# Decoder trunk: the last two sums of each scan visit on GpSimd, and dense gate and up columns side by side

## The chip, the cores and the metric

One core of a Trainium2 chip runs the whole kernel. The metric is device time in microseconds, the median of several executions. TensorE multiplies matrices, VectorE (DVE), ScalarE (ACT) and GpSimd (POOL) work elementwise, and SyncE (SP) issues the weight transfers. PSUM has eight banks of 512 float32 columns per partition.

## What is computed

Two layers of a hybrid decoder trunk over 256 tokens of width 1024. Each layer normalises its input, projects it, runs three token mixers (a diagonal state-space scan, dilated attention, attention into 256 memory tokens), merges them and adds the residual. Then comes a channel mixer: dense SwiGLU in layer 0, top-2-of-8 experts in layer 1. Two pieces matter here:

```python
def ssm_branch(u, ...):            # 32 groups x 64 complex states
    bu = jnp.einsum('blgc,gpc->blgp', uf.astype(jnp.complex64), b_bar)
    ...
    _, states = lax.associative_scan(combine, (a_el, bu), axis=1)
    y = jnp.einsum('blgp,gcp->blgc', states, c).real + d_skip * uf
...
def swiglu(h, w_gate, w_up, w_down):      # dense: 1024 -> 2816 -> 1024
    return (jax.nn.silu(h @ w_gate) * (h @ w_up)) @ w_down
```

## The kernel before

The engines run programs of their own, written out by hand, and meet at named semaphores. Matrix products of weights are split: a float32 weight tile of 128x2048 is copied by ScalarE to a rounded part `hi` (`hi_part`, line 1351), VectorE forms `lo` = tile - `hi` (`lo_part`, line 1897), and TensorE does three products per block (`split_product`, lines 583 to 585). A ring of three tiles (`ring`) is filled by SyncE (`load`, line 400), 1 MB per tile; `hi` and `lo` have three buffers each.

**The scans (`ssm`).** The states are turned into a rotating frame, scanned with real factors, and turned back. A layer has 8 visits v, each over two state blocks of 128 and both parts, real and imaginary. VectorE per visit: two products of the PSUM input with the cosine and sine tables (lines 1697, 1698, 128x1024), two sums (1704, 1705, 128x512), four scans (1708), two products to turn back (1711, 1712), two sums that write the states to `wv[v % 2]` (1713, 1714), and after some visits a skip path (1725). It waits for `states_ready` of the visit before at the head of each visit. TensorE per visit: `rotated_input(v + 1)` (line 704), one part of the input projection in plain float32 (line 618), then `state_output(v)` (line 717), which waits for `states_ready`. The input of visit v + 1 goes to the same banks as that of visit v and waits for `bu_used`.

**After the scans.** VectorE does the rotary products and head scaling, then the lo parts `ring_lo` (line 1545). ScalarE does squares of the memory keys, GELU, the key scaling (line 1241), a copy of the input, two weight copies `hi_m` (line 1110), then copies of transposed heads and the column block. GpSimd forms inverse roots (`rsqrt_mean`, lines 534 and 535): of q and k (`rqk`), then of the memory keys (`rm`). TensorE transposes the heads and goes on with split products.

**The dense part (`dense`).** The 2816 hidden columns are done in 11 blocks f of 256. A gate tile and an up tile have all 1024 rows of 256 columns each, a down tile 256 rows of 1024 columns. TensorE in the loop: gate of block f + 1 into bank 0 (two token halves of 256 columns side by side), transposes of block f's activations into bank 2, up of block f + 1 into bank 1, down of block f into banks 4 to 7. ScalarE does silu (line 1378) when gate is done, so while up is multiplied; VectorE multiplies by up (line 1936). The first block uses banks 0 and 1 for gate, 2 and 3 for up, because its first half starts before the second half of the input is transposed.

In all of it each engine takes its instructions in the order of its program.

## Time and profile before

| What | Value |
|---|---|
| Median of 3 runs | 1869.81 us (1869.48 to 1870.22) |
| Profiled execution, its own time | 1874.48 us |
| Its span from first to last instruction | 1872.6 us |
| TensorE busy | 97% |
| VectorE busy | 78% |
| ScalarE busy | 60% |
| GpSimd busy | 2% |
| Mean granted clock of TensorE | 0.988 |

The busy share counts a matmul from its start to its modelled end, and successive ones overlap; the pace is read from starts. The scans of layer 0 run from 68 to 149 us, those of layer 1 from 588 to 668, the dense part from 335 to 529, and the experts from about 870 to the end.

### The profile page before, as it was taken

How to read it: one execution, taken by the hardware profiler on the slowest of the kernel's cores; microseconds unless marked ns; L12 is line 12 of the kernel's file. 1: busy time of each engine (PE TensorE's matmuls, PEld its weight loads, DVE VectorE, ACT ScalarE, POOL GpSimd, SP SyncE). 2: the span in 40 equal slices, each digit the busy share in tenths (PEclk: the TensorE clock that was granted, in tenths of full speed). 3: DMA queues.
4: the chain of work that ended last, by engine and by line, in shares of the span. 5: the costliest groups of instructions: out<-in, count | busy, mean ns of one | idle time of the engine just before them, and what ended most of it. 6: DMA issues, size and time to landing. Idle time of an engine off the chain costs nothing.

```text
span 1872.6 us, 24006 instructions
## 1 busy us (share of the span) xinstructions
PE 1822.3 (97%) x8731; PEld 1441.1 (77%) x8731; DVE 1469.5 (78%) x1320; ACT 1130.0 (60%) x1211; POOL 43.7 (2%) x83
## 2 busy tenths in 40 slices
PE   7999999999999999998999999999999999999997
PEld 5445888999974458877888888888888888888886
DVE  7997456554469985466889898898888888988986
ACT  5336464544342364645677776776777767767774
POOL 1002000000010020000000000000000000000000
PEclk9999999999999999998999999999999999999999
DMA  6333334655543334456999999999999999999994
GB/s 215 121 113 126 128 128 154 205 176 169 194 152 113 113 113 135 127 170 228 348 369 332 370 369 329 371 349 352 373 326 365 367 338 369 350 350 369 352 372 178
DMA packets 226956, 476.48 MB, mean 254 GB/s; under 512 B 15644, under 2 KB 40344, under 8 KB 226904
## 3 DMA queue, kind: packets, MB, share of 16 engines
q1 hardware_dynamic: 226520, 474.99, 71.9%
q0 software_dynamic: 288, 0.79, 0.2%
q8 instruction: 33, 0.54, 0.1%
q14 instruction: 19, 0.16, 0.0%
q10 hardware_dynamic: 96, 0.02, 0.0%
HBM read 474.71 MB, written 1.05 MB: 254 GB/s over the span
## 4 chain that ended last, share of the span: by engine, by line
PE 60%; DVE 6%; issue 1%; ACT 0%; DVEq 0%; ACTq 0%
PE ps L583 18%; PE ps L585 18%; PE ps L584 18%; PE ps L968 2%; PE ps L989 1%; DVE z L1708 1%; DVE lo L1897 1%; DVE x L2052 1%; PE ps L784 1%; PE ps L756 1%; DVE z L1711 0%; DVE z L1698 0%; DVE z L1712 0%; PE ps L1054 0%; PE ps L1053 0%
## 5 line engine op out<-in xcount | busy, mean ns | idle before, releaser
L1897 DVE TENSOR_TENSOR lo<-ring_e,hi 128x2048 fp32r<-128x2048 f32 x336 | 767.5, 2290 | 110.8 <-ACT hi L1351 110.5
L1351 ACT ACTIVATE hi<-ring_e 128x2048 fp32r<-128x2048 f32 x336 | 644.1, 1918 | 185.3 <-PE ps L585 185.1
L583 PE MATMUL ps<-hi,xe_hi 128*128 128x512 f32 x896 | 355.6, 397 | 2.2 <-DVE lo L1897 2.0
L585 PE MATMUL ps<-hi,xe_lo 128*128 128x512 f32 x896 | 349.4, 390 | 0.0
L584 PE MATMUL ps<-lo,xe_hi 128*128 128x512 f32 x896 | 349.3, 390 | 0.0
L618 PE MATMUL ps<-ring,hT 128*128 128x512 f32 x448 | 200.7, 602 | 0.0
L583 PEld LDWEIGHTS ps<-hi,xe_hi 128*128 128x128 f32 x896 | 168.2, 188 | 39.4 <-DVE lo L1897 5.7
L585 PEld LDWEIGHTS ps<-hi,xe_lo 128*128 128x128 f32 x896 | 168.2, 188 | 36.3
L584 PEld LDWEIGHTS ps<-lo,xe_hi 128*128 128x128 f32 x896 | 168.4, 188 | 33.2
L583 PE MATMUL ps<-hi,aT_hi 128*128 128x512 f32 x464 | 181.6, 391 | 0.0
L585 PE MATMUL ps<-hi,aT_lo 128*128 128x512 f32 x464 | 180.7, 390 | 0.0
L584 PE MATMUL ps<-lo,aT_hi 128*128 128x512 f32 x464 | 180.7, 389 | 0.0
L1110 ACT ACTIVATE hi_m<-ring 128x2048 fp32r<-128x2048 f32 x52 | 99.5, 1914 | 118.4 <-PE ps L585 109.8
L618 PEld LDWEIGHTS ps<-ring,hT 128*128 128x128 f32 x448 | 84.0, 192 | 104.0 <-issue 103.9
L583 PE MATMUL ps<-hi_m,xT_hi 128*128 128x512 f32 (+1 forms) x368 | 147.1, 400 | 5.8 <-DVE ring_lo L1545 5.7
L584 PE MATMUL ps<-ring_lo,xT_hi 128*128 128x512 f32 (+1 forms) x368 | 141.3, 384 | 0.0
L1545 DVE TENSOR_TENSOR ring_lo<-ring,hi_m 128x2048 fp32r<-128x2048 f32 x52 | 118.7, 2286 | 22.5 <-ACT hi_m L1110 22.4
L585 PE MATMUL ps<-hi_m,xT_lo 128*128 128x512 f32 (+1 forms) x304 | 116.3, 382 | 0.0
L1118 ACT ACTIVATE z<-ps,rs 128x512 f32<-128x512 f32 (+1 forms) x52 | 31.9, 667 | 134.4 <-PE ps L618 134.4
L583 PE MATMUL ps<-hi,hT_hi 128*128 128x256 f32 x352 | 100.6, 286 | 1.4 <-DVE lo L1897 1.4
L585 PEld LDWEIGHTS ps<-hi,aT_lo 128*128 128x128 f32 x464 | 87.1, 188 | 18.4
L584 PEld LDWEIGHTS ps<-lo,aT_hi 128*128 128x128 f32 x464 | 87.2, 188 | 17.5
(311 smaller groups left out, 2499.4 us busy)
## 6 DMA issues: line engine op xcount, KB each, us to landing
ring_e<-in_moe_w_gate SPq DMA_DIRECT2D x112, 1024.0 KB, 6.8
ring_e<-in_moe_w_up SPq DMA_DIRECT2D x112, 1024.0 KB, 6.9
ring_e<-in_moe_w_down SPq DMA_DIRECT2D x112, 1024.0 KB, 6.6
ring<-in_w_in SPq DMA_DIRECT2D x50, 1024.0 KB, 5.1
ring<-in_ffn_w_gate SPq DMA_DIRECT2D x11, 1024.0 KB, 5.3
ring<-in_ffn_w_up SPq DMA_DIRECT2D x11, 1024.0 KB, 6.3
ring<-in_ffn_w_down SPq DMA_DIRECT2D x11, 1024.0 KB, 4.9
ring<-in_w_mem_kv SPq DMA_DIRECT2D x8, 1024.0 KB, 6.4
```

Source lines behind the costliest of these rows:

```text
L583: nc.tensor.matmul(o, x_hi, w_hi, start=first, stop=False, skip_group_check=True)
L584: nc.tensor.matmul(o, x_hi, w_lo, start=False, stop=False, skip_group_check=True)
L585: return nc.tensor.matmul(o, x_lo, w_hi, start=False, stop=end, skip_group_check=True)
L618: last = nc.tensor.matmul(o, lhs[0][:, kk, t], w[:, k, :], start=first, stop=end, skip_group_check=True)
L756: last = nc.tensor.matmul(ps[:, bank, col:col + nk], qkT[o:o + HD, 0, hd // 2, c * P:(c + 1) * P], qkT[o:o + HD, 1, hd // 2, 0:nk], start= ...
L784: last = nc.tensor.matmul(ps[:, 5, o:o + v.shape[1]], pT[:, b * P:(b + 1) * P], v, start=first, stop=end, skip_group_check=True)
L968: last = nc.tensor.matmul(ps[:, 6 + half, k % KT * P:(k % KT + 1) * P], h[:, c, k * P:(k + 1) * P], disp[:, c, :], start=c == 0, stop=c == ...
L1110: nc.scalar.activation(hi_m[:, m % 2, :], ring[:, n % R, :], ACT.Copy).then_inc(sem("mixer_hi_ready"), 1)
L1118: last = nc.scalar.activation(dst[:, c, :], ps[:, pair + c, 0:dst.shape[2]], ACT.Copy, scale=rs[:, 2 + c:3 + c])
L1351: nc.scalar.activation(hi[:, m % H, :], src, ACT.Copy).then_inc(sem("hi_ready"), 1)
L1545: V.tensor_tensor(ring_lo[:, n % R, :], ring[:, n % R, :], hi_m[:, m % 2, :].bitcast(F32), ALU.subtract).then_inc(sem("mixer_lo_ready"), 1)
L1897: last = V.tensor_tensor(lo[:, m % H, :], src, hi[:, m % H, :].bitcast(F32), ALU.subtract)
```

## The change

In the scans, VectorE's last two sums go to GpSimd. VectorE writes the cosine product to a new buffer `wc` and the sine product over `wp`, and signals `states_turned`; GpSimd forms both sums into `wv[v % 2]` and signals `states_ready`. VectorE's wait for `states_ready` of the visit before moves from the head of a visit to its scans, which overwrite `wp`.

In the dense part a tile now holds 512 of the 1024 rows, with 256 gate columns beside 256 up columns, and comes in two transfers with a semaphore each (`full`, `up_full`). One matmul covers gate and up of one row block, 512 columns wide; each token half has a bank of its own (0 and 1). The second block goes to banks 2 and 3, with the first block's transposes in bank 0. TensorE's loop is: transposes of block f, both halves of block f + 1, down of block f. Silu and product follow the end of both halves.

```diff
-        wa, wb, wp, *wv = [z[:, i // 3, SSM_COLS * BANK + i % 3 * 4 * SEQ:SSM_COLS * BANK + (i % 3 + 1) * 4 * SEQ]
-                           .rearrange("p (i r t) -> p i r t", i=2, r=2) for i in range(5)]
+        wa, wb, wp, wc, *wv = [z[:, i // 3, SSM_COLS * BANK + i % 3 * 4 * SEQ:SSM_COLS * BANK + (i % 3 + 1) * 4 * SEQ]
+                           .rearrange("p (i r t) -> p i r t", i=2, r=2) for i in range(6)]
...
                         sp.wait_ge(sem(name), count + (0 if n < BASE[1] + R else {"columns_done": COL_TILES}.get(name, MIDDLE)))
-                v = ring[:, n % R, :].rearrange("p (k n) -> p k n", n=src.shape[2])
-                sp.dma_start(v, src).then_inc(full[n % R], 16)
+                v = ring[:, n % R, :].rearrange("p (k n) -> p k n", k=blocks_ or src.shape[1])
+                sp.dma_start(v[:, :, cols_], src).then_inc(full[n % R], 16)
+                return v
...
+                    def load_pair(n, f, half, shift=0):
+                        rows = slice(half * KT * P, (half + 1) * KT * P)
+                        gate, up = (w[0][rows, bass.ds(f * 256, 256)].rearrange("(k p) n -> p k n", p=P)
+                                    for w in (ffn_gate, ffn_up))
+                        v = load(n, gate, shift, KT, slice(0, 256))
+                        sp.dma_start(v[:, :, 256:BANK], up).then_inc(up_full[n % R], 16)
...
-                    load(n0, gate_tile(ffn_gate, 0))
-                    load(n0 + 1, gate_tile(ffn_up, 0))
-                    load(n0 + 2, gate_tile(ffn_gate, 1))
-                    load(n0 + 3, gate_tile(ffn_up, 1))
+                    load_pair(n0, 0, 0)
+                    load_pair(n0 + 1, 0, 1)
+                    load_pair(n0 + 2, 1, 0)
+                    load_pair(n0 + 3, 1, 1)
                     load(n0 + 4, down_tile(0))
                     with sp.Fori(2, NF) as f:
-                        load(n0 + 5, gate_tile(ffn_gate, f), f - 2)
-                        load(n0 + 6, gate_tile(ffn_up, f), f - 2)
+                        load_pair(n0 + 5, f, 0, f - 2)
+                        load_pair(n0 + 6, f, 1, f - 2)
                         load(n0 + 7, down_tile(f - 1), f - 2)
                     load(n0 + 3 * NF - 1, down_tile(NF - 1))
...
+                for v in range(NJ // 2):
+                    w = wv[v % 2]
+                    pool.wait_ge(sem("states_turned"), NJ // 2 * l + v + 1)
+                    nc.gpsimd.tensor_tensor(w[:, :, 0, :], wc[:, :, 0, :], wp[:, :, 1, :], ALU.subtract)
+                    nc.gpsimd.tensor_tensor(w[:, :, 1, :], wc[:, :, 1, :], wp[:, :, 0, :], ALU.add).then_inc(
+                        sem("states_ready"), 1)
...
             def dense():
-                def hidden(bank, m, shift):
-                    w_hi, w_lo = split_tile(m, 256, shift)
+                def hidden(m, half, shift=0, between=None, bank=0):
+                    w_hi, w_lo = split_tile(m, BANK, shift)
                     for c in range(C):
-                        for k in range(KD):
-                            last = split_product(ps[:, bank, c * 256:(c + 1) * 256], hT_hi[:, k, c * P:(c + 1) * P],
-                                                 hT_lo[:, k, c * P:(c + 1) * P], w_hi[:, k, :], w_lo[:, k, :],
-                                                 k == 0, k == KD - 1)
+                        for k in range(KT):
+                            kk, tt = half * KT + k, slice(c * P, (c + 1) * P)
+                            last = split_product(ps[:, bank + c, :], hT_hi[:, kk, tt], hT_lo[:, kk, tt], w_hi[:, k, :],
+                                                 w_lo[:, k, :], kk == 0, kk == KD - 1)
+                        if c == 0 and between is not None:
+                            between()
                     last.then_inc(sem("split_used"), 1)
...
-                def step(f, shift, first, between=None):
-                    pe.wait_ge(sem("silu_done"), f)
-                    hidden(0, 2, shift)
+                def step(f, shift, between=None):
                     act_transposes(f)
-                    hidden(1, 3, shift)
-                    down(f, 4, shift, first, False, between)
-                def hidden_half(bank, m, half):
-                    w_hi, w_lo = split_tile(m, 256)
...
                 pe.wait_ge(sem("transposed_used"), batches_to(0, "ffn") - 2)
-                hidden_half(0, 0, 0)
-                block_pairs(x, KT, KD, (sem("x_mixed"), 1))
-                hidden_half(2, 1, 0)
+                hidden(0, 0, between=lambda: block_pairs(x, KT, KD, (sem("x_mixed"), 1)))
                 pe.wait_ge(sem("transposed_used"), batches_to(0, "ffn"))
-                hidden_half(0, 0, 1)
-                hidden_half(2, 1, 1)
-                step(1, 0, True)
+                hidden(1, 1)
+                hidden(2, 0, bank=2)
+                act_transposes(1, 0)
+                hidden(3, 1, bank=2)
+                down(1, 4, 0, True, False)
                 with pe.Fori(2, NF - 1) as f:
-                    step(f, 3 * (f - 1), False)
-                step(NF - 1, 3 * (NF - 2), False, NF)
+                    step(f, 3 * (f - 1))
+                step(NF - 1, 3 * (NF - 2), NF)
                 down(NF, FFN_TILES - 1, 0, False, True, lhs=(end_hi, end_lo))
...
-                def silu(gate_done, first=False):
+                def silu(gate_done, bank=0):
                     act.wait_ge(sem("split_used"), gate_done)
                     for c in range(C):
                         o = slice(c * 256, (c + 1) * 256)
-                        last = nc.scalar.activation(gate_act[:, o], ps[:, c, 0:256] if first else ps[:, 0, o], ACT.Silu,
+                        last = nc.scalar.activation(gate_act[:, o], ps[:, bank + c, 0:256], ACT.Silu,
                                                     scale=rs[:, 2 + c:3 + c])
                     last.then_inc(sem("silu_done"), 1)
...
-                    nc.scalar.activation(dst[:, 0:BANK], ps[:, 2, :], ACT.Copy).then_inc(sem("aT_hi_ready"), 1)
-                def step(f, s, wait_act):
-                    split(2, s)
-                    split(3, s)
-                    if wait_act:
+                    nc.scalar.activation(dst[:, 0:BANK], ps[:, bank, :], ACT.Copy).then_inc(sem("aT_hi_ready"), 1)
+                def step(f, s, first=False):
+                    if not first:
                         act.wait_ge(sem("split_used"), 3 * f - 1)
-                    act_hi(f)
+                    act_hi(f, bank=0 if first else 2)
                     split(4, s)
+                    split(5, s, pair=f + 1)
                     act.wait_ge(sem("act_ready"), f)
-                    silu(3 * f)
-                split(2, 0, False)
+                    silu(3 * f + 1, 2 if first else 0)
+                    split(6, s, pair=f + 2)
+                split(2, 0, False, 1)
                 act.wait_ge(sem("x_rs"), 2)
-                silu(1, True)
-                split(3, 0)
-                act_hi(1)
-                split(4, 0)
-                act.wait_ge(sem("act_ready"), 1)
-                silu(3)
+                silu(2)
+                split(3, 0, pair=2)
+                step(1, 0, True)
                 for k in range(KD):
                     last = nc.scalar.activation(xT_hi[:, k, :], memT[:, k, :], ACT.Copy, scale=gains[:, 1, 1, k:k + 1])
                 last.then_inc(sem("memory_hi_ready"), 1)
-                with act.Fori(2, NF) as f:
-                    step(f, f - 1, True)
+                with act.Fori(2, NF - 1) as f:
+                    step(f, f - 1)
+                act.wait_ge(sem("split_used"), 3 * NF - 4)
+                act_hi(NF - 1)
+                split(FFN_TILES - 2, 0)
+                act.wait_ge(sem("act_ready"), NF - 1)
+                silu(3 * NF - 2)
...
                     bu = ps[:, 4:6, :].rearrange("p j (r t) -> p j r t", r=2)
-                    if v > 0:
-                        dve.wait_ge(sem("states_ready"), NJ // 2 * l + v)
                     dve.wait_ge(sem("bu_done"), NJ // 2 * l + v + 1)
                     V.tensor_tensor(wa[:], bu, spread(cos, 2, 2), ALU.mult)
                     last = V.tensor_tensor(wb[:], bu, spread(sin, 2, 2), ALU.mult)
...
+                    if v > 0:
+                        dve.wait_ge(sem("states_ready"), NJ // 2 * l + v)
                     for i in range(2):
                         for r in range(2):
                             last = V.tensor_tensor_scan(wp[:, i, r, :], spT[:, 0, j + i:j + i + 1].to_broadcast([P, SEQ]),
                                                         w[:, i, r, :], 0.0, ALU.mult, ALU.add)
                     chain(last)
-                    V.tensor_tensor(wa[:], wp[:], spread(cos, 2, 2), ALU.mult)
-                    chain(V.tensor_tensor(wb[:], wp[:], spread(sin, 2, 2), ALU.mult))
-                    V.tensor_tensor(w[:, :, 0, :], wa[:, :, 0, :], wb[:, :, 1, :], ALU.subtract)
-                    V.tensor_tensor(w[:, :, 1, :], wa[:, :, 1, :], wb[:, :, 0, :], ALU.add).then_inc(
-                        sem("states_ready"), 1)
+                    chain(V.tensor_tensor(wc[:], wp[:], spread(cos, 2, 2), ALU.mult))
+                    V.tensor_tensor(wp[:], wp[:], spread(sin, 2, 2), ALU.mult).then_inc(sem("states_turned"), 1)
                     if v >= 2 and v % 2 == 0:
...
-                        last = V.scalar_tensor_tensor(out=act_out[:, o], in0=ps[:, 2 + c, 0:256] if first else ps[:, 1, o],
+                        last = V.scalar_tensor_tensor(out=act_out[:, o], in0=ps[:, bank + c, 256:BANK],
                                                       scalar=rs[:, 2 + c:3 + c],
                                                       in1=gate_act[:, o], op0=ALU.mult, op1=ALU.mult)
                     last.then_inc(sem("act_ready"), 1)
...
-                dense_product(1, 2, True)
-                def step(f, s):
-                    split(3, s)
-                    act_low(f)
+                dense_product(1, 2)
+                split(3, 0)
+                def step(f, s, first=False):
+                    act_low(f, bank=0 if first else 2)
                     split(4, s)
-                    dense_product(f + 1, 3 * f + 1)
-                step(1, 0)
+                    split(5, s)
+                    dense_product(f + 1, 3 * f + 1, 2 if first else 0)
+                    split(6, s)
+                step(1, 0, True)
                 dve.wait_ge(sem("memory_hi_ready"), 1)
                 for q in range(0, KD, 2):
                     last = memory_low(1, q)
                 last.then_inc(sem("memT_scaled"), 1)
-                with dve.Fori(2, NF) as f:
-                    split(2, f - 1)
+                with dve.Fori(2, NF - 1) as f:
                     step(f, f - 1)
+                act_low(NF - 1)
+                split(FFN_TILES - 2, 0)
+                dense_product(NF, 3 * NF - 2)
                 split(FFN_TILES - 1, 0)
                 act_low(NF, end_hi, end_lo)
                 weights_low(1, 2)
```

## Rows read from the trace of the kernel before

**Rows 1.** The page, part 1: busy time of each engine

```profile
PE 1822.3 (97%) x8731; PEld 1441.1 (77%) x8731; DVE 1469.5 (78%) x1320; ACT 1130.0 (60%) x1211; POOL 43.7 (2%) x83
```

**Rows 2.** timeline, TensorE, dense part: start, us, engine, line, shapes, [idle <-releaser]

```profile
394.84 0.28 PE L585 MATMUL ps<-hi,hT_lo 128*128 128x256 f32 x1
...
396.28 0.28 PE L585 MATMUL ps<-hi,hT_lo 128*128 128x256 f32 x1
396.40 0.40 PE L583 MATMUL ps<-hi,aT_hi 128*128 128x512 f32 x1
...
401.64 0.39 PE L585 MATMUL ps<-hi,aT_lo 128*128 128x512 f32 x1
```

**Rows 3.** timeline of ScalarE and VectorE in one dense step

```profile
497.68 0.83 ACT L1378 ACTIVATE gate_act<-ps,rs 128x256 f32<-128x256 f32 x2
...
501.08 1.92 ACT L1351 ACTIVATE hi<-ring 128x2048 fp32r<-128x2048 f32 x1 [0.77 <-PE ps L585]
...
501.17 0.88 DVE L1936 SCALAR_TENSOR_TENSOR act_out<-ps,rs,gate_act 128x256 f32<-128x256 f32 x2 [1.06 <-PE ps L585]
501.96 2.28 DVE L1897 TENSOR_TENSOR lo<-ring,hi 128x2048 fp32r<-128x2048 f32 x1
```

**Rows 4.** timeline of TensorE and ScalarE, first block of the dense part

```profile
339.75 0.39 PE L583 MATMUL ps<-hi,hT_hi 128*128 128x256 f32 x1 [0.58 <-DVE lo L1897]
...
345.85 1.28 ACT L1378 ACT_TABLE_LOAD   x1 [1.64 <-PE ps L585]
```

**Rows 5.** timeline, VectorE, one scan visit and the start of the next

```profile
98.21 1.22 DVE L1697 TENSOR_TENSOR z<-ps,costab 128x1024 f32<-128x1024 f32 x1
...
101.92 2.44 DVE L1708 TENSOR_TENSOR_SCAN z<-spT,z 128x256 f32<-128x256 f32 x4
...
106.79 0.69 DVE L1713 TENSOR_TENSOR z<-z 128x512 f32<-128x512 f32 x1
...
108.12 1.23 DVE L1697 TENSOR_TENSOR z<-ps,costab 128x1024 f32<-128x1024 f32 x1
```

**Rows 6.** timeline, TensorE: outputs (L717) and inputs (L704) of scan visits, both layers

```profile
92.27 1.06 PE L717 MATMUL ps<-z,cT 128*32 128x256 f32 x8
...
128.84 1.06 PE L717 MATMUL ps<-z,cT 128*32 128x256 f32 x8
130.62 1.14 PE L704 MATMUL ps<-uT,bT 32*128 32x256 f32 x8 [0.71 <-DVE z L1698]
...
148.42 1.06 PE L717 MATMUL ps<-z,cT 128*32 128x256 f32 x8 [1.53 <-DVE z L1714]
...
601.80 1.06 PE L717 MATMUL ps<-z,cT 128*32 128x256 f32 x8
...
668.38 1.06 PE L717 MATMUL ps<-z,cT 128*32 128x256 f32 x8 [1.53 <-DVE z L1714]
```

**Rows 7.** timeline of GpSimd, and VectorE beside it at 135.5 us

```profile
5.11 0.40 POOL L529 TENSOR_SCALAR_AFFINE_SELECT mask<-mask 128x256 f32<-128x256 f32 x1
...
136.17 0.69 POOL L534 TENSOR_SCALAR rqk<-rqk 128x48 f32<-128x48 f32 x1 [112.52 <-ACT hi_m L1226]
136.94 8.43 POOL L535 TENSOR_TENSOR rqk<-rqk,half_neg 128x48 f32<-128x48 f32 x1
...
151.24 2.36 POOL L535 TENSOR_TENSOR rm<-rm,half_neg 128x8 f32<-128x8 f32 x1
...
135.54 1.22 DVE L1712 TENSOR_TENSOR z<-z,sintab 128x1024 f32<-128x1024 f32 x1
```

**Rows 8.** timeline of ScalarE and TensorE after the scans, layer 0

```profile
161.50 1.91 ACT L1110 ACTIVATE hi_m<-ring 128x2048 fp32r<-128x2048 f32 x1 [1.44 <-DMA ring<-in_w_in]
...
169.92 0.47 PE L583 MATMUL ps<-hi_m,xT_hi 128*128 128x512 f32 x1 [0.59 <-DVE ring_lo L1545]
```

**Rows 9.** busy time by window: PE, PEld, DVE, ACT, POOL, granted clock, DMA

```profile
170.00:174.00 4.00, 4.00 (x11) 3.15 (x12) 1.98 (x1) 3.30 (x19) 0.53 (x2) 0.57 0.00 0
```

**Rows 10.** transfers by source: count, KB each, median us to landing

```profile
ring<-in_ffn_w_up SPq DMA_DIRECT2D x11, 1024.0 KB, 6.3
```

38 lines of the change are left out of this document (18 added, 20 removed).

## The prediction

> **What bounds the kernel now.** I began with the page. TensorE is busy for 97% of the span and no other engine for more than 78% [rows 1]. So a microsecond is won only where TensorE itself becomes shorter, or where it stands still. VectorE and ScalarE count only where TensorE waits for them. The change touches two places, and I read the timeline of each.
>
> In the dense part the reader should look at start times, not durations, since matmuls overlap in the records. Thirteen 256-column matmuls stand between 394.84 and 396.28 with equal steps, so one costs 1.44 / 12 = 0.120 us. The 24 matmuls of 512 columns of the down product run from 396.40 to 401.64, 5.24 / 23 = 0.228 us each [rows 2]. Twice 0.120 is 0.240: the wide form does the same columns in 0.012 us less. No gap separates them; TensorE sets the pace there. ScalarE and VectorE wait for it: 0.77 us before a hi copy, 1.06 us before the product of gate and up [rows 3].
>
> In the scans it is VectorE that sets the pace. One visit starts at 98.21, the next at 108.12, a cadence of 9.91 us without a gap [rows 5]. TensorE's share of a visit is less: from the output of visit 1 at 92.27 to that of visit 5 at 128.84 are four visits, 9.14 us each. It starts behind VectorE, catches up, and stands still in the end, 1.53 us before the last output in both layers [rows 6].
>
> **The scans, part by part.** VectorE loses the last two sums. From the first of them at 106.79 to the next visit at 108.12 are 1.33 us [rows 5], so its visit falls to 9.91 - 1.33 = 8.58 us, below TensorE's 9.14. If GpSimd keeps up, TensorE becomes the bound, and the gain is what it stands still now. Layer 0: from output 5 to output 7 it takes 148.42 - 128.84 = 19.58 us; two visits without a wait are 18.28, less the input matmuls that the last one lacks, 1.14 with its overlap, 1.07 net, 17.21. Gain 2.4 us. Layer 1: 668.38 - 601.80 = 66.58 against 7 x 9.14 - 1.07 = 62.91. Gain 3.7 us [rows 6].
>
> Does GpSimd keep up? Its sums of 128x512 with two operands have no row. The nearest is a one-operand pass over 256 columns in 0.40 us [rows 7]. Below, one sum can't be under that 0.40; above, four times its columns (512, two operands) give 1.6. I take 1.2, since part of the 0.40 is a fixed cost. The far end is the pass over 48 columns that took 0.69 [rows 7]: by width, 7.4 us per sum. I don't take it for a rate, since it began at 136.17, within VectorE's multiply that ran from 135.54 for 1.22 us, and it ended 0.10 after that one [rows 7]: it was held up.
>
> The wait for the sums moves from the head of the next visit to its scans. VectorE has 101.92 - 98.21 = 3.71 us of other work before it [rows 5]: the two products from PSUM and the two input sums. Two GpSimd sums at 1.2 plus some 0.2 for the semaphores are 2.6, so nothing waits; even at 1.6 it is 3.4. Cover is gone above 1.75 us per sum. What would queue behind the wait are the scans, the turning back, and the input matmuls of the visit after next, which need VectorE's next products. The output matmuls get their states 2.6 - 1.33 = 1.3 us later within a visit. For the last visit of layer 0: its input matmuls start at 130.62 less the 0.71 they wait now, and are done at 131.0 [rows 6]; 8.58 for VectorE and 2.6 for GpSimd give 142.2, and TensorE asks at 148.42 - 2.4 = 146.0.
>
> A rule of the Trainium skill speaks against this part. By "SBUF — State Buffer", Who interferes with whom, a VectorE instruction with two SBUF inputs contends with a GpSimd instruction that reads SBUF, and the one that comes first keeps the port for all of its duration. The held-up pass above agrees. By that rule the sums run free beside the two products that read PSUM, for 2.4 us, and the first input sum, which reads SBUF twice, starts just then: it would lose 0.1 us or nothing. The Trainium skill's "GPSIMD Engine Reference", Elementwise — side-by-side cycle accounting, gives 4497 ns for 2048 columns of such a sum; by width that is an estimate of 1.1 us for these, and with it the sum of this part stays the same.
>
> GpSimd's queue is in order, and behind the visits stand the head norms. Now the pow over q and k starts at 136.94, in the middle of the scans; then its two passes, 0.69 + 8.43, start at 142.2 and end at 151.3 [rows 7]. VectorE wants it only behind its rotary products, which start after the last output, at 147. The memory keys' norm follows: a short pass (0.4) and 2.36. It ends at 154.1, today at 151.24 + 2.36 = 153.6 [rows 7], so in layer 0 ScalarE's key scaling starts no earlier than now. In layer 1 (520 us later now, by 668.38 - 148.42) the last input matmuls end at 601.80 + 5 x 9.14 + 2.1 = 649.6, the sums at 660.8, the norm at 672.7 against 673.6: 0.9 earlier. That chain has 1.44 us of idle before its second weight copy, for a transfer that TensorE will now release earlier, and what it hands to TensorE comes 0.6 us early: TensorE's last wait before the split weights is 0.59 us, for VectorE [rows 8]. So VectorE's chain would give the whole 2.4 and 3.7, ScalarE's no more than 1.44 + 0.6 = 2.0 in layer 0 and 0.9 + 2.0 = 2.9 in layer 1. The later chain decides. Sum of the scans: 4.9 us.
>
> **The dense part, part by part.** 1056 matmuls of 256 columns become 528 of 512 (11 blocks, 48 each), on the same operands. 528 x (0.240 - 0.228) = 6.3 us [rows 2]. In the rows a fixed cost of 12 ns per matmul is what the halving saves (0.240 - 0.228). The Trainium skill's "TensorE: Matmul & The Clock Gate", Back-to-back issue gap, puts that fixed cost at 2.5 ns when the clock is warm; by it the halving would give an estimated 528 x 2.5 ns = 1.3 us.
>
> The price is that gate and up end together, so silu and product come one after the other, behind both tile halves. With T the end of the hidden product: silu 0.83, product 0.88 and semaphores, done at T + 1.9 [rows 3]. TensorE then does the down product, 24 x 0.228 = 5.5 us, and only after it wants the transposes: 3.6 us of cover. The bank that silu reads is written again only after those. The third copy of a step follows silu: hi 1.92, lo 2.28, done at T + 5.2 [rows 3], wanted at T + 11.3. Its slot is then loaded in 6.3 us [rows 10] to T + 11.5, wanted by ScalarE at T + 16.8. SyncE issues two transfers for each of 22 tiles instead of one, 22 more, of half the size and with the same row length; its queue mostly waits for lo parts, so they cost nothing while that slack of 5 us stands.
>
> The first block: TensorE's 0.58 us for the second tile's lo part [rows 4] goes, because 12 wide matmuls now stand before that tile is wanted instead of none after the transposes. In its place: tile 3's hi copy stands behind the first silu. From the end of block 0: table load 1.28 [rows 4], silu 0.83, hi 1.92, lo 2.28, semaphores 0.2, together 6.5 us; TensorE comes at 24 x 0.228 + 0.4 for the transposes = 5.9. New wait 0.6. The banks of the second block's own remove the wait for that first silu, which would be 2.2 us. At the end, the last down product waits for silu, hi, transposes and both copies in a row: by the same durations 0.1 to 0.2 us. Sum of the dense part: 6.3 + 0.6 - 0.6 - 0.15 = 6.1 us.
>
> **The sum.** 4.9 + 6.1 = 11.0 us. The profiled execution took 1874.48 us (span 1872.6), which becomes 1863.5. The median of the runs is 4.67 below it; I take the difference over: 1869.81 - 11.0 = 1858.8 us. The expert stage, the larger half of the span, keeps every instruction and only starts earlier.
>
> One cost can fall either way. At 170 us TensorE is granted 0.57 of its clock on average for 4 us, mostly the lower of its two levels [rows 9], which costs 4 x 0.43 = 1.7 us; the same spot in layer 1 keeps the full clock. The first may vanish, or the second appear: 1.7 us to both sides.
>
> **Rivals.** (a) The scans give nothing: a sum takes around 2.3 us, or the chain behind the scans swallows it. For it: the norms now queue behind the sums. Against: 3.71 us of cover, and idle in both chains. Time 1869.8 - 6.1 = 1863.7. (b) The dense part gives nothing: the wide form keeps the narrow one's pace per column, 0.240, or silu and product don't fit under the down product. Against: the wide form at 0.228 stands beside the narrow one in one stretch [rows 2], and the cover is 3.6 us. Time 1869.8 - 4.9 = 1864.9. The Trainium skill's 2.5 ns (TensorE page, as above) would put this case 1.3 us lower. (c) Slower: the sums on GpSimd become the bound. A visit is then two sums, 0.2, and 106.79 - 101.92 = 4.87 from the scans on [rows 5]. At 2.4 us per sum that is 9.9, today's cadence, and the last output also comes 2.4 + 2.4 + 0.2 - 1.33 = 3.7 later; less skips that it hides, about 2.7 per layer. So from about 2.5 us per sum the loss exceeds the dense part's 6.1. At 3 us a visit is 11.1: 8.58 + 7 x 11.1 + 6.2 = 92.5 against 80 now, 12 per layer, 1869.8 + 25 - 6.1 = 1888. The 0.69 for 48 columns speaks for it, its end just behind VectorE's against [rows 7].
>
> **How the numbers follow.** Forecast 75%, (a) 11%, (b) 9%, (c) 3%, and 2% for what I don't see. The forecast's own range takes the whole stall in both layers (1.2 more), the clock (1.7 both ways), and 0.5 to 1.5 for the small waits of the dense part: 1855.0 to 1862.5. To hold 8 in 10 with bounds it reaches to (a) and (b): 1855.0 to 1865.0. This measurement can tell about 0.2%, 3.7 us, from no change: faster is below 1866.1. All but (c) and a part of (a) and (b) lie there: faster 0.92, same 0.05, slower 0.03.
>
> **What would show it.** Right: wide matmuls 0.228 apart and steps 16.8 us apart where transposes start; GpSimd sums near 1.2 us; VectorE never waiting before a scan; outputs 9.1 us apart up to the last, at about 146.0 and 664.7; the split weights after the scans 2 to 3 us earlier. Wrong: sums over 1.75 us, VectorE's input sums stretched by the port, a wait before transposes or lo parts in each dense step, or ScalarE's key scaling late for the norm by more than its idle.

## The result and the profile after

The changed kernel takes 1855.23 us (median of 4 runs, 1853.55 to 1856.46), beside 1869.81 for the kernel before. The ratio is 0.9917, with the interval 0.9905 to 0.9929: 13.3 to 17.8 us less, where I had forecast 11.0. A second measurement of the same kernel on another chip gave 1856.21 us beside 1871.26, ratio 0.9922 (0.9908 to 0.9936). Both medians of the kernel before leave out its slow runs, one of 7232.69 us in the first measurement and two of 2027.84 and 2277.74 us in the second. Applied to the 1869.81 us of the forecast the first ratio gives 1854.3 us, 0.7 below the lower end of my range.

The profiled execution took 1854.96 us, with a span of 1853.1. The page of the changed kernel, part 1, answers to [rows 1]:

```profile
PE 1808.8 (98%) x8203; PEld 1409.6 (76%) x8203; DVE 1451.9 (78%) x1288; ACT 1130.7 (61%) x1211; POOL 81.9 (4%) x115
```

TensorE has 528 instructions fewer, VectorE 32 fewer, GpSimd 32 more. Next the timeline of TensorE, outputs of the scan visits in both layers, as in [rows 6]:

```profile
80.88 1.06 PE L730 MATMUL ps<-z,cT 128*32 128x256 f32 x8
90.00 1.06 PE L730 MATMUL ps<-z,cT 128*32 128x256 f32 x8
...
135.64 1.06 PE L730 MATMUL ps<-z,cT 128*32 128x256 f32 x8
...
585.11 1.06 PE L730 MATMUL ps<-z,cT 128*32 128x256 f32 x8
...
647.93 1.06 PE L730 MATMUL ps<-z,cT 128*32 128x256 f32 x8
```

The outputs are 9.12 us apart and none waits: TensorE sets the pace of the scans now, as forecast. From first to last are 62.8 us in both layers. One visit on GpSimd and VectorE, in place of [rows 5]:

```profile
102.41 1.27 POOL L559 TENSOR_TENSOR z<-z 128x512 f32<-128x512 f32 x1 [6.47 <-DVE z L1721]
103.64 1.27 POOL L560 TENSOR_TENSOR z<-z 128x512 f32<-128x512 f32 x1
...
103.38 1.22 DVE L1705 TENSOR_TENSOR z<-ps,sintab 128x1024 f32<-128x1024 f32 x1
104.63 0.83 DVE L1711 TENSOR_TENSOR z<-z 128x512 f32<-128x512 f32 x1
105.38 0.68 DVE L1712 TENSOR_TENSOR z<-z 128x512 f32<-128x512 f32 x1
106.09 2.44 DVE L1717 TENSOR_TENSOR_SCAN z<-spT,z 128x256 f32<-128x256 f32 x4
```

A sum takes GpSimd 1.27 us; I took 1.2. VectorE's scan waits for nothing. But its first input sum (L1711) takes 0.83 us, not 0.69: it begins at 104.63, and GpSimd's second sum runs until 104.91. That is so in four of the eight visits; in three others a skip path stands ahead of VectorE's next products, and the first has no sums beside it, and there it takes 0.69. This small delay becomes important below.

The dense part on TensorE and ScalarE, as in [rows 2, 4]:

```profile
346.18 0.50 PE L596 MATMUL ps<-hi,hT_hi 128*128 128x512 f32 x1 [0.52 <-DVE lo L1903]
...
396.76 0.39 PE L596 MATMUL ps<-hi,hT_hi 128*128 128x512 f32 x1
...
402.65 0.39 PE L598 MATMUL ps<-hi,aT_lo 128*128 128x512 f32 x1
```

```profile
339.86 1.28 ACT L1387 ACT_TABLE_LOAD   x1 [3.21 <-PE ps L598]
341.16 0.84 ACT L1387 ACTIVATE gate_act<-ps,rs 128x256 f32<-128x256 f32 x2
341.88 1.92 ACT L1358 ACTIVATE hi<-ring 128x2048 fp32r<-128x2048 f32 x1
```

The 26 steps from 396.76 to 402.65 are 0.2265 us each (5.89 / 26), and the new wait for the fourth tile, 0.6 by the forecast, is 0.52, behind table load, silu and hi copy in the order I gave. Besides that wait, the change costs time in one place, behind the scans of layer 1 (GpSimd, ScalarE, TensorE):

```profile
646.39 8.04 POOL L542 TENSOR_TENSOR rqk<-rqk,half_neg 128x48 f32<-128x48 f32 x1
654.52 0.63 POOL L541 TENSOR_SCALAR rm<-rm 128x8 f32<-128x8 f32 x1
655.23 2.23 POOL L542 TENSOR_TENSOR rm<-rm,half_neg 128x8 f32<-128x8 f32 x1
...
657.55 2.45 ACT L1246 ACTIVATE kv<-kv,rm 128x128 f32<-128x128 f32 x8 [2.31 <-POOL rm L542]
...
666.03 0.63 PE L584 MATMUL ps<-ident,kv 128*128 128x128 f32 x4 [1.35 <-ACT qkT L1091]
```

GpSimd's norms queue behind its sums, ScalarE waits 2.31 us for the last of them, and TensorE 1.35 us for ScalarE. From the last output to the first split product are 22.5 us there, 21.5 in layer 0 and in both layers of the kernel before.

### The profile page after: what moved, and what is told of

Read it like the earlier page. It is cut to its first block, busy times and chain, and to the rows that moved or that the text cites. A ratio compares the mean times of both kernels' runs of the same rounds, so it can differ in the third digit from the quotient of the medians.

```text
span 1853.1 us, 23022 instructions
## 1 busy us (share of the span) xinstructions
PE 1808.8 (98%) x8203; PEld 1409.6 (76%) x8203; DVE 1451.9 (78%) x1288; ACT 1130.7 (61%) x1211; POOL 81.9 (4%) x115
## 4 chain that ended last, share of the span: by engine, by line
PE 87%; DVE 8%; issue 2%; ACT 2%; POOL 1%; DMA 0%; DVEq 0%; ACTq 0%
PE ps L596 25%; PE ps L598 24%; PE ps L597 24%; PE ps L631 5%; PE ps L973 2%; PE ps L994 1%; PE ps L797 1%; DVE z L1717 1%; PE ps L769 1%; DVE lo L1903 1%; PE ps L584 1%; DVE x L2062 1%; PE ps L780 1%; DVE z L1720 1%; DVE z L1704 1%
## 5 line engine op out<-in xcount | busy, mean ns | idle before, releaser
L1903 DVE TENSOR_TENSOR lo<-ring,hi 128x2048 fp32r<-128x2048 f32 x33 | 75.6, 2292 | 44.0 <-ACT hi L1358 44.0
L597 PEld LDWEIGHTS ps<-lo,aT_hi 128*128 128x128 f32 x464 | 87.2, 188 | 17.8
```

The lines of the kernel that those rows point to most:

```text
L597: nc.tensor.matmul(o, x_hi, w_lo, start=False, stop=False, skip_group_check=True)
L1903: last = V.tensor_tensor(lo[:, m % H, :], src, hi[:, m % H, :].bitcast(F32), ALU.subtract)
```

## Where the time came from

The spans of the two profiled executions differ by 19.5 us, 4.9 more than the medians, since the profiled execution of the kernel before was one of its slower ones. So I compared it stage by stage with the changed kernel and three kernels of the experiments. Each stage starts where the engine that sets its pace starts (us, differences of start times):

```
stage                                   before  e4     e1     e2     after
                                                memory scans  dense
layer 0: VectorE's first product of the
  scans to first output (TensorE)       15.00   13.59  13.56  13.58  13.63
  ... to last output                    80.28   80.28  76.39  80.27  76.45
last output to first split product      21.50   21.50  21.50  21.50  21.50
first split to first hidden product    165.34  163.71 165.26 162.62 162.62
first hidden product to the down
  product behind the last one, dense   183.04  181.90 183.03 175.27 175.27
layer 1: VectorE's first product
  to first output                       13.69   12.19  13.68  13.49  12.19
  ... to last output                    80.27   80.27  76.50  80.27  75.01
last output to first split product      21.50   21.50  21.50  21.50  22.52
```

The row "to last output" is the finding. With VectorE as bound it is 80.27 or 80.28 us in every kernel with the old visit, whether TensorE's first output comes after 13.6 or after 15.0 us. With TensorE as bound it is the first output plus 62.8. In the profiled execution of the kernel before TensorE had a lower granted clock shortly ahead of both scans (a cold stretch, below), and was late. Busy time by window of the kernel before (columns as in [rows 9]):

```profile
36.00:44.00 8.00, 8.00 (x27) 6.12 (x28) 7.56 (x21) 2.44 (x7) 0.00 (x0) 0.79 0.26 100
...
588.00:600.00 12.00, 9.49 (x21) 4.42 (x22) 11.77 (x15) 7.51 (x4) 0.00 (x0) 0.72 0.23 86
```

and of the kernel of e4, which is the kernel before but for its memory copies:

```profile
36.00:44.00 8.00, 8.00 (x31) 5.54 (x31) 7.61 (x22) 2.80 (x6) 0.00 (x0) 1.00 0.45 156
588.00:592.00 4.00, 4.00 (x11) 1.70 (x8) 3.93 (x7) 4.00 (x4) 0.00 (x0) 0.58 0.02 4
592.00:600.00 8.00, 8.00 (x31) 3.59 (x30) 7.81 (x11) 0.60 (x2) 0.00 (x0) 1.00 0.17 44
```

My stall of 2.4 us was measured from an output that was itself 1.4 us late (15.00 against 13.59). The lateness cost the kernel before nothing, as VectorE's chain covered it, and so TensorE stood still that much less. By the stages the scans give 80.28 - 76.45 = 3.8 us in layer 0. In layer 1 they give 3.8 if TensorE is late there (e1), or 5.3 less the 1.0 behind the scans, 4.2, if not. The dense part gives 183.04 - 175.27 = 7.8. Together 15.4 to 15.8 us, against 14.6 and 15.1 between the medians. The rest of the 19.5 us belongs to the two executions, not to the change: 2.7 between the first split and the first hidden product of layer 0, where the granted clock of the kernel before was 0.79 and 0.78 from 168 to 176 us and 0.95 and 0.63 from 276 to 284, and 0.9 ahead of the scans. The first of these stages took 162.6 us in e2, 163.7 in e4 and 165.3 in e1 and in e10, so it goes with neither part of the change.

## The experiments

Ratios are to the kernel before on the same chip; intervals are 95%. Kernels e1 to e4 ran together, e5 to e8, and e9 to e12.

**e1: the scan part alone.** The kernel before with only the scan part of the change, its new buffer, its semaphore and the moved wait included. Its core:

```
-  V.tensor_tensor(w[:, :, 0, :], wa[:, :, 0, :], wb[:, :, 1, :], ALU.subtract)
-  V.tensor_tensor(w[:, :, 1, :], wa[:, :, 1, :], wb[:, :, 0, :], ALU.add)
+  nc.gpsimd.tensor_tensor(w[:, :, 0, :], wc[:, :, 0, :], wp[:, :, 1, :], ALU.subtract)
+  nc.gpsimd.tensor_tensor(w[:, :, 1, :], wc[:, :, 1, :], wp[:, :, 0, :], ALU.add)
...
```

> The kernel before with the scan part of the change alone (GpSimd forms the two last sums). Theory A (the parts are independent, and the scan part gives the net shifts that the changed kernel's trace showed, 2.46 us at the last output of layer 0 and 2.74 us up to the first product after the scans of layer 1): 5.1 us less, ratio 0.997 to the kernel before. Theory B (part of the gain of the whole change comes from TensorE's granted clock, or from the parts together, which neither part has alone): under 4 us or over 6.5 us less, with the cold stretches of this run elsewhere than at 170 and 280 us. GpSimd's sums 1.27 us each, VectorE's visit 8.7 us, outputs of the products 9.13 us apart in both.

Measured: 1863.88 us, ratio 0.9961 (0.9947 to 0.9974), 7.3 us less; 7.6 between the medians. Theory A's 5.1 is just inside the interval (4.9 to 9.9), but what it rests on was wrong: it took the shifts from the first output on. The stages of the table give 3.9 + 3.8 = 7.7. The size is theory B's, over 6.5, but not its cause: where the kernel before has a low granted clock at 168 and 276 us, this one has it at 164 and 272, the same places of its program, and between its first split and first hidden product it takes 165.26 us against 165.34. The gain is in the two scan stages.

**e2: the dense part alone.** The tile order, the 512-column products and the banks of the second block, on the kernel before.

> The kernel before with the dense part of the change alone (gate and up columns side by side, second block in banks of its own). Theory A (independent parts): 9 steps by 0.59 us from the wide products is 5.3, the wait of 0.87 to 1.17 us behind the memory copies in the second step gone, 1.3 in the first two blocks: 7.8 us less, ratio 0.996. My forecast's own sum for this part was 6.1 (ratio 0.9967). Theory B: what the measured 14.6 us holds beyond 5.1 + 7.8 = 12.9 is found here, 9 to 10 us less, if the clock of the dense part is what rose.

Measured: 1863.30 us, ratio 0.9964 (0.9950 to 0.9977), 6.7 us less by the ratio and 8.2 by the medians. Its stage is 175.27, as that of the whole change. The two parts add up: 7.7 and 7.8 in the traces, and 1 - 0.9961 + 1 - 0.9964 = 0.0075 against 0.0083 measured for both.

**e3: narrow products in the new order.** In the changed kernel each hidden product becomes two:

```
+  for n in range(2):
+      o = slice(n * 256, (n + 1) * 256)
+      ... split_product(ps[:, bank + c, o], ..., w_hi[:, k, o], w_lo[:, k, o], kk == 0 and n == 0, ...)
```

> The changed kernel with each 512-column hidden product of the dense part issued as two of 256 columns, gate and up, in the same banks and order of tiles. Theory A (a product costs its columns plus a fixed part of about 12 ns, so 528 more of them cost it 528 times): 5.3 to 6.4 us more than the changed kernel, ratio to the kernel before about 0.995. Rival (the gain of the dense steps came from the order of the tiles and the banks, not the width; fixed part of 2.5 ns): 0 to 1.3 us more than the changed kernel, ratio 0.992 to 0.993, and steps of the dense part within 0.15 us of 16.82 us.

Measured: 1862.52 us, ratio 0.9953 (0.9940 to 0.9967), 7.3 us over the changed kernel's first median and 6.3 over its second. The stage is 181.54 us, 6.3 more. In it TensorE's wait ahead of the fourth tile is 0.20 us, not 0.52, so that the products themselves cost 6.6 more, and 6.59 / 528 = 12.5 ns each. TensorE's timeline of this kernel, dense part:

```profile
395.78 0.28 PE L596 MATMUL ps<-hi,hT_hi 128*128 128x256 f32 x1
...
399.98 0.28 PE L598 MATMUL ps<-hi,hT_lo 128*128 128x256 f32 x1
```

That is 35 steps of 0.120. The width is the gain; the 2.5 ns that the rival took is not what is seen here. (The Trainium skill's "TensorE: Matmul & The Clock Gate", Back-to-back issue gap, gives that figure for the isolated gap, and says that in a stream of weight loads and products both set the spacing. These products have weights of their own each, and the trace shows 12.5 ns.)

**e4: the memory's copies spread over two steps.** In the kernel before:

```
-  for k in range(KD): last = nc.scalar.activation(xT_hi[:, k, :], memT[:, k, :], ...)
+  for part_ in range(2):
+      for k in range(part_ * KT, part_ * KT + KT): last = nc.scalar.activation(...)
+      if part_ == 0: step(2, 1, True)
...
```

VectorE's low parts of the memory are spread in the same way.

> The kernel before with the copies of the memory (high part on ScalarE, low part on VectorE) spread over two dense steps, four and four, in place of all eight in one. Theory (the wait of 0.87 us of TensorE for the low copies of a hidden tile, in the second dense step, comes from VectorE forming the memory's low copies for 3.25 us just before; the step has no other cause for it): the wait goes, 0.9 to 1.2 us less than the kernel before, ratio 0.9994. Rival (the wait comes from the tile's late load or from ScalarE's high copies, which are the same work in either place): the wait stays, no change within 0.3 us.

Its reason is a wait that I had missed. VectorE and TensorE in the kernel before, second dense step:

```profile
361.43 3.25 DVE L1563 SCALAR_TENSOR_TENSOR mem_lo<-memT,par,xT_hi 128x256 fp32r<-128x256 f32 x8
364.59 4.49 DVE L1897 TENSOR_TENSOR lo<-ring,hi 128x2048 fp32r<-128x2048 f32 x2
...
366.93 0.39 PE L583 MATMUL ps<-hi,hT_hi 128*128 128x256 f32 x1 [0.87 <-DVE lo L1897]
```

Measured: the wait is gone and the stage 181.90 us in place of 183.04, 1.1 less. The time, 1870.92 us, ratio 0.9996 (0.9987 to 1.0005), can't show so little. In the changed kernel the wait is gone too, since a step there is 12 wide products ahead of the next tile.

**e5 and e6: three and four sums per visit.** In the changed kernel GpSimd's first sum is done twice, or three times:

```
+  chain(nc.gpsimd.tensor_tensor(w[:, :, 0, :], wc[:, :, 0, :], wp[:, :, 1, :], ALU.subtract))
```

> The changed kernel with GpSimd's first sum of each visit done twice over: three sums in place of two. Theory A (cover of 3.7 us between VectorE's last product of a visit and its next input sum, and a visit that may last up to TensorE's 9.13 us): three sums with their wait take 3.9 to 4.0 us, VectorE waits 0.2 to 0.3 us, the visit lasts at most 9.0 us, outputs stay 9.13 us apart, under 1 us more than the changed kernel. Rival (the sums already bound the visit, as the rival of the prediction has it): 1.27 us by 16 visits by 2 layers less the first, 30 to 40 us more.

> The changed kernel with GpSimd's first sum of each visit done three times over: four sums in place of two. Theory A: the sums take 5.2 us or more against a cover of 3.7, the visit grows to about 10.2 us and passes TensorE's 9.13, so 7 visits by 1.1 us in each layer, 8 to 10 us at each last output: 15 to 20 us more than the changed kernel, outputs of the products 10.2 us apart. Rival (GpSimd's sums have more cover than 3.7 us, or VectorE doesn't wait for them): under 5 us more, outputs still 9.13 us apart.

Measured: e5 1876.81 us, ratio 1.0028 (1.0017 to 1.0039), 21.6 us over the changed kernel; e6 1895.76, ratio 1.0129 (1.0114 to 1.0145), 40.5 over. My theory fell: a third sum already costs more than the whole change gives. The rival's size, 30 to 40 us, wasn't met either. By the stages of the table, e5 loses 6.0 and 7.4 us up to the last outputs and 4.4 and 3.4 behind them. VectorE doesn't wait for the third sum by a semaphore. Its own sum stands still. VectorE and GpSimd in e5:

```profile
97.13 1.21 DVE L1706 TENSOR_TENSOR z<-ps,sintab 128x1024 f32<-128x1024 f32 x1
98.37 1.78 DVE L1712 TENSOR_TENSOR z<-z 128x512 f32<-128x512 f32 x1
100.08 0.68 DVE L1713 TENSOR_TENSOR z<-z 128x512 f32<-128x512 f32 x1
...
97.11 1.27 POOL L560 TENSOR_TENSOR z<-z 128x512 f32<-128x512 f32 x1
98.34 1.27 POOL L561 TENSOR_TENSOR z<-z 128x512 f32<-128x512 f32 x1
```

GpSimd's third sum starts at 98.34, VectorE's first input sum at 98.37; it takes 1.78 us in place of 0.69 and ends at 100.15, 0.54 after GpSimd's. VectorE's product before it, with one operand in PSUM, ran its 1.21 us undisturbed beside the second sum. Outputs are (149.64 - 80.80) / 7 = 9.83 us apart in layer 0. In the visits in between both engines delay each other: VectorE's sums take 0.95 and 1.75 us and GpSimd's third takes 1.71. With four sums GpSimd's last two take up to 1.72 us, and VectorE's scan does wait, 1.22 us; outputs are 11.04 us apart, where I expected 10.2.

So the cover of the changed kernel isn't the 3.71 us up to the scans but the 2.2 us up to VectorE's first input sum (104.63 less 102.41), and two sums of 1.27 exceed it already, by 0.28 us, except where a skip path adds its 0.4 us to the cover. The Trainium skill's "SBUF — State Buffer", Who interferes with whom, has this rule: a VectorE instruction with two SBUF inputs and a GpSimd instruction that reads SBUF exclude each other, and the first to start keeps the port. For sums the trace agrees to 0.15 us: 0.69 us after GpSimd's end would be 100.30, and VectorE's sum ended at 100.15. I had applied it to two sums alone, and not to the threshold of 1.75 us per sum.

**e7: the second block in the banks of the first.** In the changed kernel:

```
-  hidden(2, 0, bank=2)
+  pe.wait_ge(sem("act_ready"), 1)
+  hidden(2, 0)
...
```

> The changed kernel with the second dense block in the banks of the first, so that its first product waits until ScalarE and VectorE have read these banks. Theory A (banks of its own cover that reading, as the part of the change says): a wait of about 3.3 us ahead of the second block, 0.5 us of a later wait for the tile's low copies goes, 2.8 us more than the changed kernel. Rival (TensorE has other work there, or the wait only replaces the later one for the low copies): under 0.7 us more.

Measured: 1861.19 us, ratio 0.9949 (0.9935 to 0.9963), 6.0 over the changed kernel's first median, 5.0 over its second. TensorE's timeline, and the windows behind it:

```profile
344.39 0.50 PE L596 MATMUL ps<-hi,hT_hi 128*128 128x512 f32 x1 [3.28 <-DVE act_out L1943]
```

```profile
344.00:348.00 4.00, 3.61 (x10) 2.88 (x11) 2.63 (x2) 1.13 (x1) 0.00 (x0) 0.66 0.40 137
348.00:352.00 4.00, 4.00 (x20) 3.23 (x19) 0.00 (x0) 0.00 (x0) 0.00 (x0) 0.91 0.78 241
```

The wait is 3.28 as expected here (the prediction had 2.2 for it, as it counted silu and not VectorE's product, which reads these banks too), but the stage grows by 4.4 and not by 2.8. After the wait the granted clock is 0.66 and 0.91 for 4 us each: 4 x (0.34 + 0.09) = 1.7 us. In the changed kernel this place keeps the full clock. Another such stretch at 272 to 280 us explains 1.2 more.

**e8: half of the inverse roots.** GpSimd's power over 48 columns becomes one over 24 and a plain product over 24. Half of the query and key norms are left out by it.

> The changed kernel with GpSimd's inverse roots of the query and key norms formed for one half of the columns alone; the other half is left as a plain product, so that these norms aren't the reference's. It shortens the 8.0 us instruction behind the last sums to about 4.0. Theory A (after the scans of layer 1 ScalarE waits 2.3 us for the memory's key norm, which stands behind that instruction on GpSimd, and TensorE's transposes wait 1.35 us for ScalarE): both waits go, 1.0 us less than the changed kernel, all of it in layer 1. Rival (ScalarE's chain there ends with VectorE's copies, so that the norm's delay is hidden): no change within 0.3 us.

Measured: 1856.10 us, ratio 0.9919 (0.9906 to 0.9933), no change that can be told. In the trace both waits are gone, and from the first output of layer 1 to the first product after the scans are 84.32 us, not 85.34: 1.0 less. But this doesn't show theory A yet. The execution had a granted clock of 0.50 to 0.84 from 572 to 584 us, where the changed kernel has 0.59 for 4 us; TensorE's first output was 1.2 us late by it (13.42 against 12.19), and VectorE and GpSimd were that much ahead. e7, with all its powers and a first output at 13.71, has 84.32 us too, and ScalarE waits only 0.56 there. The clean comparison is e10.

**e9: a power in place of the third sum.** In the changed kernel, behind the two sums:

```
+  nc.gpsimd.tensor_tensor(spare[:, 1, 0:6], spare[:, 0, 0:6], half_neg[:, 0:6], ALU.pow).then_inc(
+      sem("states_ready"), 1)
```

> The changed kernel with a third GpSimd instruction behind the two sums of each visit that takes about as long as a sum (estimate 1.3 us: 4.19 us for 24 columns and 8.04 us for 48 give 0.16 a column and 0.34 besides) but reads 6 columns of a spare tile in place of 512: a power. The next scan waits for it as it waited for the third sum. Theory A (in the run with three sums VectorE's two-input sums stood still until GpSimd's sum beside them had ended, because both read whole tiles of SBUF; a power, which beside VectorE's sums in the kernel before left them at 0.69 us, doesn't do that): VectorE's input sums stay at 0.69 to 0.85 us, the scans wait 0.2 to 0.5 us, the visit lasts at most 9.1 us, outputs about 9.13 us apart, under 3 us more than the changed kernel. Rival (any GpSimd instruction that reads SBUF holds VectorE's sums for its whole length, or the delay was the wait for the third instruction): the visit passes 9.9 us as with three sums, VectorE's sums 1.7 us, 15 to 22 us more.

Measured: 1870.71 us, ratio 0.9993 (0.9984 to 1.0003), 14.5 over the changed kernel beside it. VectorE's sums behaved as theory A has it, the waits and the time did not. VectorE and GpSimd:

```profile
97.39 0.72 DVE L1714 TENSOR_TENSOR z<-z 128x512 f32<-128x512 f32 x1
98.03 0.68 DVE L1715 TENSOR_TENSOR z<-z 128x512 f32<-128x512 f32 x1
98.79 2.44 DVE L1720 TENSOR_TENSOR_SCAN z<-spT,z 128x256 f32<-128x256 f32 x4
...
108.18 2.44 DVE L1720 TENSOR_TENSOR_SCAN z<-spT,z 128x256 f32<-128x256 f32 x4 [0.69 <-POOL spare L563]
...
97.36 1.33 POOL L563 TENSOR_TENSOR spare<-spare,half_neg 128x6 f32<-128x6 f32 x1
...
106.41 1.66 POOL L563 TENSOR_TENSOR spare<-spare,half_neg 128x6 f32<-128x6 f32 x1
```

The power lasts as long as a sum and reads SBUF, and VectorE's sums beside it stay at 0.72 and 0.68. So it isn't GpSimd's instruction as such that stops VectorE, nor the wait for a third one. The kernel before has a power over 48 columns from 136.94 to 145.37 us, and VectorE's sums at 140.87 and 141.48 took 0.69 each beside it. Whether the operation makes the difference, or that it reads few columns in its time, isn't shown. The Trainium skill's rule ("SBUF — State Buffer", Who interferes with whom), which has the port held for the whole instruction, doesn't hold for these powers. In four of the visits of each layer the power took 1.66 us and the scan waited 0.7 for it, more than the 0.5 I had allowed. The last output comes 1.0 us later in layer 0 (144.66), 0.7 more in layer 1. The rest is lost behind the scans, on ScalarE and TensorE:

```profile
157.01 2.16 ACT L1249 ACTIVATE kv<-kv,rm 128x128 f32<-128x128 f32 x7 [5.94 <-POOL rm L544]
...
165.48 1.02 PE L587 MATMUL ps<-ident,kv 128*128 128x128 f32 x4 [4.08 <-ACT qkT L1094]
```

VectorE's visits now last 9.2 us in the mean, where they were 8.8 in the changed kernel and TensorE's are 9.1, so VectorE no longer runs ahead. The last sums start at 140.71, not at 137.81, the norms behind them start 4.3 us later, and TensorE loses 3.8 us in layer 0 and 2.7 in layer 1. That makes 8.2 of the 14.5; in this execution three cold stretches (at 164, 580 and 676 us) add about 4. Up to the difference from the other executions, some 2 us, this stays open.

**e10 and e11: two improvements, tried.** Half of the inverse roots ahead of the last visit's sums (e10), and a one-column silu that loads ScalarE's table early (e11, both together):

```
+  if v == NJ // 2 - 1:
+      ... nc.gpsimd.tensor_tensor(flat(rqk2)[:, 0:24], flat(rqk)[:, 0:24], half_neg[:, 0:24], ALU.pow)
...
+  nc.scalar.activation(gate_act[:, 0:1], half_pi[:], ACT.Silu)
```

> The changed kernel with the first half of GpSimd's inverse roots for the query and key norms moved ahead of the sums of the last scan visit, into the 6.2 us in which GpSimd is idle there. Nothing is left out. Theory: as in the run with half of the powers the wait of 2.31 us of ScalarE and that of 1.35 us of TensorE behind the scans of layer 1 go, and that stretch (first output of the scans to the first product after them) gets 1.0 us shorter; the sums of the last visit aren't delayed (power 4.2 us in a gap of 6.2). Time 0 to 1 us less than the changed kernel, as far as the clock lets it be seen. Rival: the power beside VectorE's sums, or the sums behind the power, delay the last visit and the stretch stays or grows.

> The kernel of the run with the split inverse roots, and ScalarE loads the table of its gate function (1.28 us) by a one-column instruction ahead of the first dense tile's wait, in its idle time there. Theory: the hidden tile's high copy is 0.5 to 1.3 us earlier, and TensorE's wait of 0.52 us for the low copy of the third dense tile goes: 0.5 us less than the run before this one. Rival: VectorE's own copies set that wait, no change.

Measured: e10 1856.36 us, ratio 0.9917 (0.9903 to 0.9931); e11 1855.89, ratio 0.9918 (0.9904 to 0.9932); the changed kernel beside them 1856.21. In the traces both do what they should. In e10 TensorE's first output of layer 1 comes as in the changed kernel (12.19 us), ScalarE's wait for the norm and TensorE's for ScalarE are gone, and the stretch to the first split product is 84.3 us, 1.0 less. In e11 the wait of 0.52 us is gone and the dense stage is 174.53, 0.7 less. The times can't tell 1.7 us, so neither is a version that has been shown to be faster.

**e12: the changed kernel again.**

> The changed kernel as it is, beside the two variants and the kernel before on one chip. By the first measurement: 14.6 to 15.5 us less than the kernel before, ratio 0.9905 to 0.9929. If what it gains beyond 13.0 us of waits and products is chance in the granted clock of single executions, its trace shows cold stretches in other places than the first one did, and the time from landmark to landmark agrees with that trace wherever neither is cold.

Measured: 1856.21 us, ratio 0.9922 (0.9908 to 0.9936). This second trace agrees with the first to 0.02 us in all stages of the table from first output to last and in the dense part, and has its cold stretches of the first 800 us at the same two places, from 12 to 20 and from 576 to 580 us. So by this test the gain over 13.0 isn't a chance of the first execution. The stages named its cause instead.

## Why the prediction was off by 4 us

The mechanisms held: VectorE's visit fell below TensorE's, GpSimd's sums fit, the wide products gave their fixed cost, the new wait of 0.5 us came where I put it. The held-up pass was read rightly too: it takes 0.24 us in the changed kernel, where VectorE stands idle beside it, not 0.69. The sum of 11.0 us was too small, the stages give 15.4 to 15.8, and it failed in three terms.

**The stall of the scans, 2.4 and 3.7 us.** It was read as TensorE's waits in one execution [rows 6], and TensorE's first outputs were late in it. The size is 3.8 and 3.8 to 5.3. I looked for a low granted clock behind the scans [rows 9] and left a charge of 1.7 us to both sides for it, but not ahead of them, where it hides a stall.

**"The later chain decides": 2.0 and 2.9 instead of 2.4 and 3.7.** In layer 0 nothing was taken off: the first split product moved by the same 4.72 us as the last output (169.92 to 165.20, 148.42 to 143.70). The step that failed is the time of GpSimd's norms: I had the last sums end at 142.2 and the memory keys' norm at 154.1, so that ScalarE's key scaling started no earlier than before. They ended at 140.30 and 151.49. I had counted from the last input products of the trace before, whose TensorE was late (end at 131.0, against 128.6 in the changed kernel), and GpSimd's two passes over q and k took 8.4 us, not 9.1. So the key scaling started at 151.58 in place of 154.03, the idle 1.44 us went, and ScalarE's second weight copy ended 4.0 us earlier. In layer 1 the loss was right in kind and about in size, 1.0 us for my 0.8, through the wait of 2.31 us for the memory key's norm; e10 takes it away, and where TensorE's first output is late (e1, e7) it doesn't arise. In both layers together the scans give 7.6 to 8.1 us, not 4.9.

**The dense part, 6.1 us.** The wide form gave 6.6 for my 6.3, as e3 measures. Missing was the wait of 0.87 us behind VectorE's memory copies, worth 1.1 (e4). My small waits, -0.15 together, came to +0.1: 0.58 went, 0.52 came, and the 0.1 to 0.2 at the end isn't seen. Sum 7.8.

**What the forecast said of its rivals.** (a) and (b), that one part gives nothing, are excluded by e1 and e2. (c), GpSimd's sums as the bound, was described rightly in its effect but its point was wrong. VectorE's input sum already stands still for 0.14 us with two sums of 1.27, in four of eight visits, and its visits, 8.6 to 9.1 us and 8.8 in the mean, leave 0.3 to TensorE's 9.1; so an estimate is (2 x 1.27 + 0.3) / 2 = 1.4 us per sum, not 1.75. By it VectorE would have been the bound again at my upper bound of 1.6, where I wrote that nothing waits; e5, with 3.8 us of sums, shows what that leads to. I had also left the skip path out of VectorE's visit: with it the kernel before has 10.05 us in the mean, not 9.91.

**The clock.** In single executions the granted clock still decides over 1 to 5 us: the runs of the kernel before on one chip went from 1869.18 to 1874.35 us, the highest at a mean of 0.988. Where it falls isn't settled. It fell beside or after waits of 3.3 (e7) and 4.0 to 4.3 us (TensorE's first input product of layer 1, in every trace), but also at 36 us in one execution of the kernel before and not in the next kernel's.

## What to carry to other kernels

When a stage passes from one engine to another as its bound, measure it from where the old bound starts, not by the waits of the new one: a profiled execution in which the new bound happened to be late hides a part of the stall (here 1.4 us in layer 0 and 1.5 in layer 1). When work goes from VectorE to GpSimd, the cover ends at VectorE's next instruction with two SBUF operands, not at the first that needs the result; count up to there. And a matmul has a fixed cost worth counting: 528 fewer, of twice the width, gave 6.6 us.

## What the runs showed of the hardware

A GpSimd sum of two 128x512 operands takes 1.27 us. Beside it VectorE's sum of two SBUF operands stands still until it ends (0.69 becomes 1.78), a VectorE product with one operand in PSUM doesn't (1.21), and a GpSimd power of 1.33 us (e9) or 8.43 us (the kernel before) leaves VectorE's sums alone. The other way round GpSimd is held as well: its pass over 8 columns took 1.36 us in e9 while VectorE multiplied from SBUF, and ended 0.06 after the last of these products; the same pass took 0.20 where VectorE stood idle. A wait of TensorE can cost half as much again in clock behind it (e7, one trace: 3.3 us of wait, 1.7 us of clock).
